# Prompt attention: where the weighting of the three branches' outputs stands between the units of the loop

## The reference, cut to what matters

```
    o_cmp, p_cmp = cmp_attention(q, pos, kc, vc)                            # k = 0, compressed keys
...
        o_slc = slc_attention_blocked(q_rot, pos, idx, ks_blk, vs_blk)      # k = 1, selected blocks
        o_win = win_attention_banded(q_rot, win_rows[:, :, 0], win_rows[:, :, 1])   # k = 2, window of 512
...
    g3 = jax.nn.sigmoid(cg).reshape(B, T, 3, C_HEADS, 1)
    oc = g3[:, :, 0] * o_cmp + g3[:, :, 1] * o_slc + g3[:, :, 2] * o_win
    yc = oc.reshape(B, T, C_WIDTH).astype(x.dtype) * jax.nn.silu(cz)
```

## Time and profile before

| | us |
|---|---|
| median of 3 runs | 1710.97 |
| lowest, highest | 1709.56, 1711.38 |
| the profiled execution's own time | 1710.52 |
| its span (first to last instruction) | 1708.7 |
| busy in the span: PE, DVE, ACT, POOL | 1563.6, 879.5, 561.3, 472.2 |

### The profile page before, as it was taken

The page is one execution under the profiler, slowest core; times in us unless marked ns, Lnnn a source line. Parts: engine busy times, 40 slices in busy tenths (PEclk is TensorE's granted clock), DMA queues, the critical chain, the costliest instruction groups (busy, mean ns, idle before and its releaser), DMA issues.

```text
span 1708.7 us, 32992 instructions
## 1 busy us (share of the span) xinstructions
PE 1563.6 (92%) x13388; PEld 1391.4 (81%) x13388; DVE 879.5 (51%) x1515; ACT 561.3 (33%) x1109; POOL 472.2 (28%) x461
## 2 busy tenths in 40 slices
PE   7799988988888999999988998999899998999997
PEld 3699975666666888888878998898789987999997
DVE  1552366666653133332332337776772376457587
ACT  0312135555442223332311145446352566000100
POOL 1103101000002112111122158677673122235600
PEclk9899999999998999999998999999999999999999
DMA  9322120000004524444224211112032110644422
GB/s 298 116 86 63 27 88 1 1 1 1 1 2 120 149 82 131 122 130 117 66 80 149 87 51 51 57 47 75 27 103 77 29 53 26 210 162 141 146 88 87
DMA packets 136841, 143.04 MB, mean 84 GB/s; under 512 B 17110, under 2 KB 126706, under 8 KB 135922
## 3 DMA queue, kind: packets, MB, share of 16 engines
q1 hardware_dynamic: 127698, 127.19, 24.4%
q10 hardware_dynamic: 8992, 13.74, 2.3%
HBM read 115.62 MB, written 29.40 MB: 85 GB/s over the span
## 4 chain that ended last, share of the span: by engine, by line
PE 51%; DVE 9%; ACT 6%; issue 2%; DMA 1%; POOL 0%; SPq 0%; DVEq 0%; ACTq 0%; POOLq 0%
PE ps L1014 41%; PE ps L1315 2%; DVE xq L2452 1%; ACT xq L1953 1%; PE ps L1328 1%; PE ps L1510 1%; DVE att L2469 1%; ACT srw L1872 1%; ACT L1852 1%; PE ps L1606 1%; DVE sel L2336 0%; PE ps L1517 0%; DVE acc L2621 0%; DVE ab L2435 0%; DMA yst<-y_spill 0%
## 5 line engine op out<-in xcount | busy, mean ns | idle before, releaser
L1014 PE MATMUL ps<-w_hi,h_hi 128*128 128x256 f32 x792 | 229.7, 290 | 6.7 <-DVEq L152 2.9
L1014 PE MATMUL ps<-w_lo,h_hi 128*128 128x256 f32 x792 | 225.1, 284 | 0.0
L1014 PE MATMUL ps<-w_hi,h_lo 128*128 128x256 f32 x792 | 224.9, 284 | 0.0
L1014 PE MATMUL ps<-h_hi,w_hi 128*128 128x344 f32 x600 | 200.3, 334 | 4.8 <-POOL w_lo L906 1.8
L1014 PE MATMUL ps<-h_lo,w_hi 128*128 128x344 f32 x600 | 194.3, 324 | 0.0
L1014 PE MATMUL ps<-h_hi,w_lo 128*128 128x344 f32 x600 | 193.9, 323 | 0.0
L1014 PE MATMUL ps<-h_hi,wg_hi 128*128 128x344 f32 x432 | 145.8, 338 | 16.4 <-ACT gate_stage L1826 15.5
L1014 PEld LDWEIGHTS ps<-w_hi,h_hi 128*128 128x128 f32 x792 | 152.2, 192 | 8.8 <-DVEq L152 3.3
L1014 PEld LDWEIGHTS ps<-w_lo,h_hi 128*128 128x128 f32 x792 | 152.2, 192 | 0.0
L1014 PEld LDWEIGHTS ps<-w_hi,h_lo 128*128 128x128 f32 x792 | 152.1, 192 | 0.0
L905 POOL CAST w_hi<-w_raw 128x1024 fp32r<-128x1024 f32 (+1 forms) x48 | 53.7, 1120 | 338.1 <-DMA w_raw<-in_w_in 143.7
(11 more groups left out here) (456 smaller groups left out, 3519.1 us busy)
## 6 DMA issues: line engine op xcount, KB each, us to landing
w_raw<-in_w_in SPq DMA_DIRECT2D x46, 512.0 KB, 4.9
sgm<-gate_spill SPq DMA_DIRECT2D x22, 516.0 KB, 6.4
gate_spill<-gate_stage ACTq DMA_DIRECT2D x54, 172.0 KB, 2.2
w_raw<-in_w_in SPq DMA_DIRECT2D x34, 256.0 KB, 4.4
adw<-in_ada_w SPq DMA_DIRECT2D x8, 1024.0 KB, 11.1
pgc<-in_cache_nsa_kv SPq DMA_DIRECT2D x64, 128.0 KB, 2.8
pg<-in_cache_nsa_kv SPq DMA_DIRECT2D x64, 128.0 KB
w_raw<-in_w_branch SPq DMA_DIRECT2D x12, 512.0 KB, 5.7
```

Source lines behind the costliest of these rows:

```text
L1014: last = mm(out, lhsT=l, rhs=r, start=(first and i == 0 and j == 0), stop=(final and i == n - 1 and j == 2), skip_group_check=joint)
```

## The change

`o_out` gets a second argument that says which of the two halves to do; the wait for the output, 1/sum and the weight go with the first half. The calls are laid out anew: branch 0 is put on a list at the end of the turn where it was done before, and its two halves are done in the next two turns; branch 1 is put on the list in its turn, its first half done at once and its second in the next turn. Branch 2 stays in one piece at its place. The computation is the same.

```diff
-        def o_out(u):
+        def o_out(u, halves):
...
             n = oi - t - 1
-            if k and n >= 2:
-                v.wait_ge(e("to_added"), n - 1)
-            for gg in range(2):
+            if 0 in halves:
+                if k == 0:
+                    v.wait_ge(e("pv_done"), u + 1)
+                else:
+                    v.wait_ge(e("o_turned"), 2 * t + k)
+                st(V.reciprocal(w, SM[:, t % 2, 8 * k:8 * k + 8]))
+                st(tt(w.rearrange("p (h g) -> p h g", g=2), w.rearrange("p (h g) -> p h g", g=2),
+                      G3[:, t, 8 * k:8 * k + 8].rearrange("p (g h) -> p h g", g=2), MUL))
...
+                if k and n >= 2:
+                    v.wait_ge(e("to_added"), n - 1)
+            for gg in halves:
...
         maxes(0)
+        later = []
         for u in range(NU + 2):
             if u + 1 < NU:
                 maxes(u + 1)
             if u < NU:
                 tv_out(u)
-            if group_end(u - 2):
-                o_out(u - 2)
+            if group_end(u - 2) and AU[u - 2][0] == 1:
+                later += [(u - 2, 0), (u - 2, 1)]
+            if group_end(u - 2) and AU[u - 2][0] == 2:
+                o_out(u - 2, (0, 1))
+            elif later:
+                done, half = later.pop(0)
+                o_out(done, (half,))
             if 1 <= u <= NU and AU[u - 1][0] == 0:
-                o_out(u - 1)
+                later += [(u - 1, 0), (u - 1, 1)]
```

More of the change, by code:

```diff
@@ L2244, in tv_out @@
                 st(V.reduce_sum(SM[:, t % 2, 0:8], PR[:, u % 2, 0:512].rearrange("p (h c) -> p h c", c=64), AX))
-        def o_out(u):
+        def o_out(u, halves):
             k, t, hh, k0, n = AU[u]
             oi = 3 * t + k
[L2249 to L2252, removed]
             bank = 6 + oi % 2
             w = CW[:, 8:16]
[L2255 to L2260, removed]
-            n = oi - t - 1
-            if k and n >= 2:
-                v.wait_ge(e("to_added"), n - 1)
-            for gg in range(2):
+            n = oi - t - 1
+            if 0 in halves:
[6 more added lines that the diff above has]
+                      G3[:, t, 8 * k:8 * k + 8].rearrange("p (g h) -> p h g", g=2), MUL))
+                if k == 0 and t == 0:
+                    st(ts(w, w, G[:, GRV:GRV + 1], None, MUL))
+                if k and n >= 2:
+                    v.wait_ge(e("to_added"), n - 1)
+            for gg in halves:
                 src = ps[:, bank, :].rearrange("p (a b g d) -> p a b g d", a=2, b=2, g=2)[:, :, :, gg, :]
```

## The result

The changed kernel takes 1689.46 us (median of 4 runs, 1686.52 to 1695.4), beside 1711.18 for the kernel before, run next to it on the same chip. The ratio is 0.988, its 95% interval 0.985 to 0.991: faster by 21.7 us, 1.3%. That is 6.5 us under the forecast of 1696 and 1.5 under the low end of its range. Later runs, some of them on other chips, put the same kernel a little higher. All 12 executions of it together have the median 1692.0 us (1686.5 to 1695.7), 37 of the kernel before 1710.7 (1701.1 to 1715.7). By these the change is worth 18.7 us.

The account below looks back on a forecast made before the run. No engine is full; DVE's late row extremes at round boundaries make ACT and PE wait. 13.45 - 0.2 + 1.6 = 14.85 us off 1710.52 gives 1695.7; with medians 0.45 higher, 1696 us, range 1691 to 1702.

Parts of the forecast that it names:

- The mechanism at the boundary: Round boundary: branch 0's weighting on DVE delays the next row extremes by 2.35 us; moving it out gains 13.45 us over eight rounds.
- The two views that bracketed rounds 4 to 6: Wide rounds: ACT's idle time (2.03, 1.06, 1.44 us) and PE's gap (2.33, 1.81, 2.10) bracket gains of 2.0, 1.4, 1.8.
- The hold: Round boundary, rounds 1 to 6: POOL's addition holds branch 0's 8-column product on DVE about 1.0 us, inside the 2.35 us.
- The pieces: Branch 0's halves in the next two units, 0.9 and 0.45 us, fit DVE's idle time; 0.2 us off for rounds 1 and 2.
- Branch 1: Its second half, one unit later, puts 0.45 us before a unit's extremes; hidden, counted as nothing, bound 1.4 us.
- Rival C: Round boundary: DVE's copy of a portion is held beside POOL's addition instead, 1.4 us less gain, 1697.5 us; chance 0.03.
- Rival A: Attention stage: same gain, but the slow clock stays or moves to another gap; 1697.7 us, 1699.3 with another stretch; chance 0.25.
- Rival B: Round boundary: branch 2's own weighting becomes the bound or the pieces lie half bare; gain 9.6 us, 1701.4 us; chance 0.12.
- D: Slower: pieces delay extremes needed at once and the boundary is freed for nothing; 10.8 us lost, 1721.8 us; chance 0.04.
- E: No change: the old turn already waited for something else; within 0.2% of 1711 us; chance 0.03.
- The clock: Behind PE's gap in round 3, the stretch at the lower clock goes with the gap: 1.6 us, bounds 0 and 3.2.
- A little for the clock behind the stage: After the attention stage: an allowance that took the range's low end from 1692.6 to 1691 us.

## Why the prediction was off

**The mechanism at the boundary was right, and its sizes nearly so.** By how much the time from the start of a round to the start of the next fell, for each round between two executions that met the same clock in it:

| round | 0 | 1 | 2 | 3 | 4 | 5 | 6 | 7 | sum |
|---|---|---|---|---|---|---|---|---|---|
| forecast | 0.7 | 2.25 | 2.25 | 2.35 + 1.6 | 2.0 | 1.4 | 1.8 | 0.5 | 14.85 |
| measured | 0.66 | 2.1 | 2.5 | 3.9 | 2.15 | 1.26 | 1.6 | 0.67 | 14.8 |

(the 0.1 for the late extremes is taken from rounds 1 and 2, and round 3 has the slow stretch of the earlier trace rows in both lines). That the sums agree to 0.1 us is luck. In round 0 the 0.66 is one pair of three; pairs with more slow time in it give 0.5 and 0.13. Without the 1.7 us of the slow stretch the measured line is 13.1, and the means over all executions at full clock give 12.75. The two views that bracketed rounds 4 to 6, ACT's idle time and PE's gap, held them: 2.15 between 2.03 and 2.33, 1.26 between 1.06 and 1.81, 1.6 between 1.44 and 2.10.

**The hold** was 1.0 us in six places, as put, and it is gone. It lies inside the 2.35, as the prediction had it. With 6.0 of 12.75 us it is nearly half of what the boundary gave.

**The pieces** behave as put: the extremes behind the first one are 0.16 us late in round 2 (put as 0.2, of which 0.1 counted), and behind the second DVE waits. **Branch 1** was counted as nothing and is nothing. **Rival C** fails: a copy lies beside POOL's addition for 0.50 us and takes 0.68 as everywhere. The Trainium skill, "SBUF — State Buffer", section "Who interferes with whom", says that copies can be locked out by GpSimd when their operands meet its conditions; this one, out of PSUM, isn't, while the product of 8 columns with both inputs in SBUF was held for 1.0 us. **Rival A** had the slow stretch of round 3 stay or move to another gap; in the four executions of the changed kernel there is none between 252 and 469 us. The one of round 7 stood in all three executions of the kernel before already, and stands in three of the four. **Rival B** asked for 9.6 us, **D** for a slower kernel and **E** for no change; none of them is there.

**The step that failed is the clock**, in two terms.

The term in the stage was too small. "The clock" took off 1.6 us, one stretch, with 3.2 as its bound. The slow time in the stage is 12.0, 16.9 and 13.7 us in the three executions of the kernel before, mean 14.2, and 3.4, 6.7, 8.7 and 8.7 in the four of the changed one, mean 6.9. Half of the difference is 3.65 us. Nearly all of it is the stretches in rounds 1 to 3: two of 3.4 us on average before, none after, which makes 3.4 us of time, where 1.6 stood in the sum. The slow time at the start of round 0 is 4 us on average in both kernels. The trace of before happened to be the one with the fewest such stretches: "equal gaps in rounds 1 and 2 brought no such stretch" was true of that execution and false of the next two. By the Trainium skill, "TensorE: Matmul & The Clock Gate", section "HAM oscillation — how this bites in real kernels", idle time between bursts throttles PE again when it is long enough. The prediction left the condition out and read from it that the drop goes for certain with its gap. The traces show that it went: where the gaps are gone, so are the stretches, in ten executions of ten. They also show that a gap of 2.43 to 2.53 us need not bring one: 8 of 12 did.

The term behind the stage was missing. "A little for the clock behind the stage" was 1.6 us at the low end of the range and nothing in the sum. There the slow time goes from 55.6 to 69.2 us between executions of one and the same program, that is 6.8 us of time, and 1.7 us of gain go with the changed kernel by the shorter first stretch, in all of its executions; by what cause is open.

The sum with the measured terms: the stage 12.75 at full clock (forecast 13.25) and 3.65 by its clock, 16.4; 1.7 by the first stretch behind it; together 18.1, where the pooled runs give 18.7. The remaining 0.6 is less than they can tell. The forecast was 14.85, so 3.85 us are missing from it: 0.5 too much in the gaps, 2.05 too little for the clock in the stage, 1.7 for the stretch behind it and 0.6 open. The last 2.5 us, from the 1692.0 of all twelve executions to the first median of 1689.46, are taken as chance: four executions that lay 9 us apart. The pooled median is inside the range of 1691 to 1702; the first median isn't, since the range had no room for the scatter of a median of four.

## What to carry to other kernels

Look at what is placed between a producer and a consumer that waits, and ask of each instruction there who needs its result: the one nobody waits for moves out, and the ones on which an engine waits stay whole (branch 2's halving lost 7.8 us). Before moving a chain, look at the durations of one line, least against most: a row of 167/168/1167 ns says that something may hold it, the order of time says what ran beside it, and moving two small instructions in front of that neighbour gave two thirds of the gain. Compare two traces stage by stage after taking off half of the time at the lower clock, and profile the old kernel more than once before a term of a forecast rests on which gap the clock answered.

## What the runs showed of the hardware

A product of two SBUF operands of 8 columns on DVE took 0.167 us alone. When it began inside POOL's addition, it ended with it, 0.4 to 1.0 us later. In the four executions with branch 0 at its old place and in the one with branch 2 halved, that is so of all 28 that met an addition, and the other products of this line took 0.17. What decided wasn't the size: 1/sum, as small but with a single SBUF input, took its usual 0.19 us wholly inside an addition. The halves with an operand in PSUM (0.88 us) and the copy out of PSUM (0.68) weren't lengthened either.

The clock was the surprise. The same program met a gap of 2.53 us and kept its clock in one execution and lost it in the next; a gap of 2.33 us in round 4 was never followed by a slow stretch, and one of 2.00 us in round 7 was in all three executions of the kernel before and in three of four of the changed one. So the length of a gap alone doesn't decide; what does isn't shown. Over the span, such differences go with a scatter of the times of one program of 3 us to either side (standard deviation 3.3 us over 37 executions of the kernel before, 2.9 over 12 of the changed one, on several chips).
